# A down projection of 22 k-tiles rewritten as Strassen's seven block products

## The reference

```python
def conv_glu_ffn(h, w_up, conv_w, conv_b, w_down):
    a = h @ w_up
    ...
    gate, val = jnp.split(c, 2, axis=-1)
    return (jax.nn.silu(gate) * val) @ w_down
...
x = x + conv_glu_ffn(rmsnorm(x, ffn_norm_g[l]), ...)
```

## Time and profile before

| | us |
|---|---|
| median of three runs | 2753.74 |
| span of the profiled execution | 2752.7 |
| PE busy | 2696.4 |
| DVE busy | 1451.5 |
| POOL busy | 1127.4 |
| ACT busy | 1068.8 |

### The profile page before, as it was taken

One profiled execution on the slowest core, in us unless ns is written; L12 is line 12 of the kernel. 1 busy time (PEld: TensorE's weight loads), 2 busy tenths in 40 slices (PEclk: granted clock), 3 DMA queues, 4 the chain that ended last, 5 costly groups with the idle time before them and its releaser, 6 DMA issues.

```text
span 2752.7 us, 34759 instructions
## 1 busy us (share of the span) xinstructions
PE 2696.4 (98%) x13662; PEld 2197.4 (80%) x13662; DVE 1451.5 (53%) x2038; ACT 1068.8 (39%) x1614; POOL 1127.4 (41%) x625
## 2 busy tenths in 40 slices
PE   8999999999999999999999999999998999999998
...
GB/s 152 31 40 75 101 106 54 25 30 114 71 77 84 77 84 77 192 174 139 122 74 68 67 72 65 70 65 66 65 100 85 39 39 39 39 39 39 39 54 164
DMA packets 111787, 214.24 MB, mean 78 GB/s; under 512 B 32032, under 2 KB 61888, under 8 KB 111504
## 3 DMA queue, kind: packets, MB, share of 16 engines
...
q0 software_dynamic: 448, 1.88, 0.2%
...
## 4 chain that ended last, share of the span: by engine, by line
PE 88%; DVE 5%; ACT 2%; issue 2%; DMA 1%; POOL 1%; SPq 0%; ACTq 0%; DVEq 0%; POOLq 0%
PE gemm L1011 21%; PE gemm L1012 20%; PE gemm L1013 20%; PE small L1193 2%; PE small L1736 2%; PE small L1013 2%; PE small L1012 2%; PE small L1011 2%; PE small L1724 1%; PE small L1581 1%; PE gemm L1134 1%; PE small L1306 1%; PE small L1326 1%; PE gemm L1137 1%; PE gemm L1138 1%
## 5 line engine op out<-in xcount | busy, mean ns | idle before, releaser
L1011 PE MATMUL gemm<-h_hi,w_hi 128*128 128x512 f32 x2136 | 894.6, 419 | 22.7 <-DVE h_lo L2722 8.9
L1012 PE MATMUL gemm<-h_lo,w_hi 128*128 128x512 f32 x2136 | 845.1, 396 | 0.0
L1013 PE MATMUL gemm<-h_hi,w_lo 128*128 128x512 f32 x1960 | 776.6, 396 | 0.0
L819 POOL TENSOR_TENSOR w_hi<-w_raw,unit_col 128x1024 fp32r<-128x1024 f32 x134 | 262.6, 1960 | 1134.4 <-PE gemm L1013 891.6
L1011 PEld LDWEIGHTS gemm<-h_hi,w_hi 128*128 128x128 f32 x2136 | 403.9, 189 | 106.5 <-issue 11.2
L1012 PEld LDWEIGHTS gemm<-h_lo,w_hi 128*128 128x128 f32 x2136 | 404.3, 189 | 74.8 <-issue 2.9
L1013 PEld LDWEIGHTS gemm<-h_hi,w_lo 128*128 128x128 f32 x1960 | 369.3, 188 | 89.6
L828 POOL TENSOR_TENSOR w_lo<-w_raw,w_hi 128x1024 fp32r<-128x1024 f32 x118 | 305.3, 2587 | 13.8 <-DVE w_lo L2881 4.9
L972 POOL TENSOR_TENSOR w_hi<-w_raw,unit_col 128x1024 fp32r<-128x1024 f32 x32 | 60.8, 1899 | 310.9 <-PE gemm L1013 310.9
L3080 DVE TENSOR_TENSOR t_lo<-t_lo_f,t_hi 128x1024 fp32r<-128x1024 f32 x36 | 44.5, 1282 | 143.1 <-ACT t_hi L2238 143.1
L2541 ACT ACTIVATE xres<-xres,stat 128x128 f32<-128x128 f32 (+3 forms) x64 | 49.7, 777 | 151.0 <-DVE stat L3553 150.7
...
## 6 DMA issues: line engine op xcount, KB each, us to landing
w_raw<-w_stream SPq DMA_DIRECT2D x178, 512.0 KB, 3.5
t_lo_f<-act_spill SPq DMA_DIRECT2D x36, 512.0 KB, 4.4
act_spill<-taps SPq DMA_DIRECT2D x22, 512.0 KB, 2.9
x_spill<-xres ACTq DMA_DIRECT2D x16, 512.0 KB, 2.7
v_gate<-w_stream SPq DMA_DIRECT2D x11, 512.0 KB, 4.2
v_val<-w_stream SPq DMA_DIRECT2D x11, 512.0 KB, 3.4
xres<-x_t SPq DMA_DIRECT2D x8, 512.0 KB, 8.7
xres<-x_t ACTq DMA_DIRECT2D x8, 512.0 KB, 4.9
```

What stands on the lines that cost most here:

```text
L819: nc.gpsimd.tensor_tensor(whi[d][:, :, :], raw[s][:, :, :], unit, ALU.mult).then_inc(w_hi_done, 1)
L1011: mm(dst, w_hi, a_hi, start=first, stop=False, skip_group_check=onto)
L1012: mm(dst, w_hi, a_lo, start=False, stop=False, skip_group_check=onto)
L1013: return mm(dst, w_lo, a_hi, start=False, stop=last, skip_group_check=onto)
```

## The change

The down projection becomes one Strassen step over 2x2 blocks: the output features are cut in two halves, the tokens in two halves of 512, and the 22 k-tiles in 11 and 11. A unit `u` (0 to 10) is one k-tile of each half. There are seven block products. Each takes 11 units of 12 matmuls: four output tiles times the three of `dot3`, over 512 tokens. They run in four groups: two products side by side in groups 0, 1 and 2, one in group 3. TensorE goes (u, first), (u-1, second), (u+1, first), and so on, and keeps the first product's sums in four half banks (`A_BANKS`) and the second's in four others (`B_BANKS`). `unit_mm` counts finished units; the buffers of a unit are three deep, and most writes for unit n wait for `unit_mm` n-2, the end of unit n-3.

For each unit of groups 0, 1, 2, 3 POOL forms 1, 2, 1, 1 sums of weight blocks in place and 2, 1, 2, 0 low parts; ACT rounds each weight and each activation operand; DVE forms 1, 2, 1, 0 sums of activations, the low part of each activation operand in groups 0 to 2, and 0, 1, 0, 1 low parts of weights. In group 2 DVE also makes the sum and the low part for group 3's activations (`down_late_sum`, `down_late_low`). All of these are 128x512. At the end of each product `bank_add` adds each of four half banks to one or two places of `xres` (`TARGETS`). Weights are loaded anew for every group, 11, 17, 11 and 11 loads of 512 KB, into six buffers (four others in group 3); the activations are loaded once, in strips of 512 tokens. The GDN weights' first two splits wait for `unit_mm` 33.

```diff
+UNITS = FF_STEPS
+N_TWO = 3 * UNITS
+N_RAW, N_LATE = 6, 4
+W_SUMS, T_SUMS = (1, 2, 1, 1), (1, 2, 1, 0)
+POOL_LOWS, DVE_LOWS = (2, 1, 2, 0), (0, 1, 0, 1)
...
+        TARGETS = {(0, 0): ((C21, ALU.add), (C22, ALU.subtract)), (0, 1): ((C11, ALU.add), (C21, ALU.add)),
+                   (1, 0): ((C11, ALU.add), (C22, ALU.add)), (1, 1): ((C22, ALU.add),),
+                   (2, 0): ((C12, ALU.add), (C22, ALU.add)), (2, 1): ((C11, ALU.subtract), (C12, ALU.add)),
+                   (3, 0): ((C11, ALU.add),)}
+        ORDER = [(UNITS * g + u - part, part) for g in range(GROUPS - 1) for u in range(UNITS + 1) for part in range(2)
+                 if 0 <= u - part < UNITS]
...
+            def raw_load(j):
+                g, v, (i, a) = RAW_LOADS[j]
+                b, before = raw_of(j), raw_before(j)
+                if j < 2:
+                    sp.wait_ge(*prod_mm(PRODUCTS * (PAIRS - 2) + (3, 7)[j]))
+                elif j == 3:
+                    sp.wait_ge(*ff_scaled(2 * PAIRS))
+                elif j in (4, 5):
+                    sp.wait_ge(ff_prod, PAIRS)
+                if before is not None:
+                    _, used = units_of(*RAW_LOADS[before][0:2])
+                    sp.wait_ge(*w_a_ready(sums_to(POOL_LOWS, used)))
+                    if used > UNITS:
+                        sp.wait_ge(*w_b_ready(sums_to(DVE_LOWS, used)))
+                elif j >= N_EARLY:
+                    sp.wait_ge(*t_ready(t_place(2 * UNITS + CUT, 0)))
+                sp.dma_start(RAWS[b], w_stream[down_at(i, a)]).then_inc(raw_in[b].sem, 16)
...
+            act_load(R2, (0, 4), (SECOND[0], 0), b21_in[0])
+            raw_load(3)
             act_store(PAIRS - 1)
+            act_load(R2, (4, 8), (SECOND[4], 0), b21_in[1])
+            for j in (4, 5, 6, 7):
+                raw_load(j)
...
+            for n in range(N_UNITS):
+                g = n // UNITS
+                for half_row in SLABS[g]:
+                    raw_wait(n, *half_row)
+                if g == 0:
+                    down_sum(n, (0, 1), (1, 1), (0, 1), ALU.add)
+                elif g == 1:
+                    down_sum(n, (0, 0), (1, 1), (1, 1), ALU.add)
+                    down_sum(n, (0, 1), (0, 0), (0, 1), ALU.subtract)
+                elif g == 2:
+                    down_sum(n, (1, 0), (0, 0), (1, 0), ALU.add)
+                else:
+                    down_sum(n, (1, 0), (1, 1), (1, 0), ALU.subtract)
+                    continue
+                for part in range(POOL_LOWS[g]):
+                    pool.wait_ge(*w_rounded(2 * n + part + 1))
+                    nc.gpsimd.tensor_tensor(dw_low(n, part), dw_value(n, part), dw_hi(n, part).bitcast(F32), ALU.subtract).then_inc(w_a_ready.sem, 1)
+            pool.wait_ge(unit_mm, N_TWO)
...
+                    if u == 0 and g:
+                        bank_free(pe, g - 1, part, q)
+                    elif u == 0 and part == 0:
+                        pe.wait_ge(ff_prod, PAIRS - 1) if q < 2 else pe.wait_ge(*ff_scaled(2 * PAIRS))
+                    elif u == 0:
+                        pe.wait_ge(ff_prod, PAIRS - 1) if q < 2 else pe.wait_ge(*ff_scaled(2 * PAIRS - 1))
+                    last = dot3((A_BANKS, B_BANKS)[part][q], dw_hi(n, part)[:, q, :], dw_low(n, part)[:, q, :], dt_hi(n, part), dt_low(n, part),
+                                u == 0, u == UNITS - 1)
+                    if u == UNITS - 1 and (q < 3 or (part == 0 and g < GROUPS - 1)):
+                        last.then_inc(bank_mm.sem, 1)
...
+            for g in range(GROUPS):
+                for u in range(UNITS):
+                    unit_products(UNITS * g + u, 0)
+                    if u and g < GROUPS - 1:
+                        unit_products(UNITS * g + u - 1, 1)
+                if g < GROUPS - 1:
+                    unit_products(UNITS * g + UNITS - 1, 1)
...
+                    act.wait_ge(*prod_mm(PRODUCTS * (PAIRS - 1) + ((2, 4), (5, 6))[n][part]))
+                elif (n, part) == (2, 1):
+                    act.wait_ge(*ff_scaled(2 * PAIRS))
+                elif 3 <= n < N_TWO:
+                    act.wait_ge(unit_mm, n - 2)
+                elif n >= N_TWO:
+                    act.wait_ge(unit_mm, N_TWO - 1 if u < 3 else n - 2)
+                A(dw_hi(n, part), dw_value(n, part), ACT.Copy).then_inc(w_rounded.sem, 1)
...
+            down_t_high(0, 1)
             tap2(PAIRS - 1, 1)
+            down_w_high(2, 0)
+            down_t_high(2, 0)
+            down_w_high(2, 1)
+            down_t_high(1, 1)
             gate(PAIRS - 1)
+            for n in range(3, N_TWO):
+                g, u = divmod(n, UNITS)
+                if u == 0:
+                    down_t_high(n - 1, 1)
+                down_w_high(n, 0)
+                down_t_high(n, 0)
+                down_w_high(n, 1)
+                if u:
+                    down_t_high(n - 1, 1)
...
+                V.tensor_tensor(dt_value(n, part), left, right, op).then_inc(t_summed.sem, 1)
+                V.tensor_tensor(dt_low(n, part), dt_value(n, part), dt_hi(n, part).bitcast(F32), ALU.subtract).then_inc(t_ready.sem, 1)
...
+                V.tensor_tensor(dw_low(n, part), dw_value(n, part), dw_hi(n, part).bitcast(F32), ALU.subtract).then_inc(w_b_ready.sem, 1)
...
+                V.tensor_tensor(B21[u], B21[u], B22[u], ALU.add).then_inc(late_sum.sem, 1)
...
+                V.tensor_tensor(B21_r[u], B21[u], B22_r[u].bitcast(F32), ALU.subtract).then_inc(late_ready.sem, 1)
...
+                bank = (A_BANKS, B_BANKS)[part][q]
+                for i, ((m, c), op) in enumerate(TARGETS[g, part]):
+                    acc = xres[:, m + q, half(c)]
+                    ready = (g, part, i) in ((2, 0, 1), (3, 0, 0))
+                    V.tensor_tensor(acc, acc, bank, op).then_inc(down_ev if ready else bank_out.sem, 1)
...
+                    down_t_low(1, 0)
+                    down_t_sum(0, 1)
+                    down_t_low(0, 1)
                 tap(p, 0, 1)
                 tap(p, 0, 0)
+                if p == PAIRS - 1:
+                    down_t_sum(1, 1)
+                    down_t_low(2, 0)
                 tap(p, 1, 1)
+                if p == PAIRS - 1:
+                    down_t_low(1, 1)
                 tap(p, 1, 0)
                 product(p)
...
+            for n in range(3, N_TWO):
+                g, u = divmod(n, UNITS)
+                if u:
+                    down_t_sum(n, 0)
+                down_t_sum(n - 1, 1)
+                if u == 0:
+                    down_t_sum(n, 0)
+                    down_t_low(n - 1, 1)
+                down_t_low(n, 0)
+                if u:
+                    down_t_low(n - 1, 1)
+                if DVE_LOWS[g]:
+                    down_w_low(n)
+                if g == GROUPS - 2 and u >= 2:
+                    down_late_sum(u - 2)
+                if g == GROUPS - 2 and u >= 3:
+                    down_late_low(u - 3)
+                for part in range(2):
+                    if g and u == part:
+                        for q in range(4):
+                            bank_add(g - 1, part, q)
+            last = GROUPS - 2
+            down_t_low(N_TWO - 1, 1)
+            for u in range(UNITS - 2, UNITS):
+                down_late_sum(u)
+            down_w_low(N_TWO)
+            for u in range(UNITS - 3, UNITS):
+                down_late_low(u)
+            for q in range(4):
+                bank_add(last, 0, q)
+                if q % 2:
+                    down_w_low(N_TWO + 1 + q // 2)
+            for q in range(4):
+                bank_add(last, 1, q)
+                if q % 2:
+                    down_w_low(N_TWO + 3 + q // 2)
+            for u in range(5, UNITS):
+                down_w_low(N_TWO + u)
+                if u < 5 + KT // 2:
+                    lo_gained(u - 5)
+            for q in range(4):
+                bank_add(GROUPS - 1, 0, q)
+            for k in range(KT // 2, KT - 1):
+                lo_gained(k)
```

More of the change, by code:

```diff
@@ L107 @@
 IN_STREAM = 2 * PAIRS
+SKIP = IN_STREAM + 2 * FF_STEPS
 def up_at(u):
@@ L227, in build @@
         sum_w = sb("sum_w", [P, KT, 2])
+        w_ex = sb("w_ex", [P, KT, P], F32R)
+        with nc.sbuf_tensor("h_hi_f", [P, KT, S], F32) as hhi_f:
+            pass
         hhi = sb("h_hi", [P, KT, S], F32R)
@@ L258, in build @@
         H = sb("head", [P, 4, S])
+        with nc.sbuf_tensor("norm_r", [P, 4, S], F32R) as N_r:
+            pass
         N = sb("norm", [P, 4, S])
@@ new lines, in t_sums, with w_sums, bank_count @@
+        def t_sums(n, part):
+            return sum(summed(m // UNITS, at) for m, at in ORDER[:t_place(n, part)])
+        def w_sums(n, part):
+            g, u = divmod(n, UNITS)
+            return sum(W_SUMS[:g]) * UNITS + W_SUMS[g] * u + (1 + part if g == 1 else 1)
+        def bank_count(g, part, q):
+            done = 0
+            for key in TARGETS:
+                each = 1 if key == (2, 0) else len(TARGETS[key])
+                if key == (g, part):
```

(20 more changed lines are left out.)

371 lines of the change are left out of this document (235 added, 136 removed).

## The result

Four executions of the changed kernel gave 2778.07 to 2789.12 us, a median of 2783.21 us; four of the kernel before gave 2750.53 to 2758.90 us, a median of 2754.53 us. The ratio is 1.0101, 95% interval [1.0083, 1.0119]. The change makes the kernel 1% slower. The forecast of 2754.0 us was wrong, and the time lies above the range of 2734 to 2773 us. The medians differ by 28.7 us.

What follows compares the result with a forecast made beforehand. PE's matmul count bounds the stage, after the change DVE and POOL's turns in groups 1 and 2. Savings of 32.5 us against losses summed to +0.3 us on the span, so 2754.0 us; range 2734 to 2773 us.

Steps and rivals of the forecast that it cites:

- 132 matmuls fewer: Down projection: 924 matmuls stand for 1056, one every 0.2334 us, 30.8 us less.
- P (wait of 1.74 us gone): P, the end of the up products, moves from 1117.3 to 1115.6 as PE's wait for DVE goes: -1.7 us.
- start, clock with it: Start of the down projection: unit 4 late through product and loads, 9.4 us lost, plus 0.8 for a lower clock.
- group 1: Second group: DVE and POOL taking turns, 6.24 us a unit, 72.5 us against 61.6 of matmuls; loss 9.5 us.
- group 2: Third group: DVE and POOL taking turns, 70.1 us against 61.6 of matmuls; loss 8.5 us.
- border 2 to 3: From T, the end of group 2's last product: bank additions begin at T+0.4 and free banks late; loss 3.5 us.
- E to the norm's reciprocal: Behind E, the first GDN matmul: three lo_gained are left after the last matmul instead of one; loss 1.1 us.
- rival C: Group 3: weight loads late, turnover 13.5 us for 11.2, +7, 2761 us; chance 0.09 together with a start at its upper bound.
- A: Rival for groups 1 and 2: turns fit beside the matmuls, PE stays the bound; -15.2, 2738.5 us; chance 0.31.
- B: Rival for groups 1 and 2: DVE-POOL pairs cost full durations, 1.98 us; +21.7, 2775 us; chance 0.20, down to half its size.
- plus 1.2 as before: Group 2: 1.2 us added, as in group 1, for moments when DVE waits for ACT and POOL has nothing to do.
- 0.8 + 3 x 1.2: End of the stage: three lo_gained left put line 3134 at 4.3 us behind the last matmul, before 3.2; loss 1.1.

Runs made afterwards that it cites:

- Experiment 1: Changed kernel with POOL's sums and low parts in groups 1 and 2 a quarter as wide, the rest left out: 2750.68 us, 0.9979 of the kernel before.
- experiment 2: Changed kernel with DVE's down_late_sum ahead of down_t_low in group 2: 2776.37 us, 1.0065 of the kernel before.
- Experiment 7: Changed kernel with the last pair's taps and product ahead of units 1 and 2's sums and low parts, gate ahead of roundings: 2775.34 us, ratio 1.0069.
- Experiment 12: Changed kernel with late sum, last product and loads 4 and 5 earlier, own B21 semaphore, POOL's sums 34 to 36 held: 2769.05 us, ratio 1.0042.
- experiment 8: Changed kernel with the first two GDN weight tiles loaded early and split by POOL behind its fourth sum of group 3: 2785.12 us, ratio 1.0104.

## Why the prediction was wrong

The sum, step by step, on the profiled executions. At 0.2334 us a matmul a unit takes 5.60 us, a group of 22 products 61.62 us, and the 924 matmuls 215.7 us; P to E has 50.8 us more than that.

| term | forecast | measured |
|---|---|---|
| 132 matmuls fewer | -30.8 | -30.8 |
| P (wait of 1.74 us gone) | -1.7 | -4.3 |
| start, clock with it | +10.2 | +15.6 |
| rest of group 0 | 0 | +0.6 |
| group 1 | +9.5 | +12.9 |
| group 2 | +8.5 | +14.9 |
| border 2 to 3 | +3.5 | +6.9 |
| group 3 | 0 | -0.2 |
| E to the norm's reciprocal | +1.1 | +5.6 |
| all behind that | 0 | +2.4 |
| sum | +0.3 | +23.6 |

**What was right.** The matmuls kept their pitch but for 3% (0.231 us apart in group 0 without waits, 0.227 in group 3), the wait ahead of the last up product went, group 0 ran at the matmuls' pace, and in groups 1 and 2 the bound was DVE and POOL taking turns, 1.70 us a pair for the 1.68 of the forecast. Experiment 1 shows it: with short POOL operations 28.8 us went. Group 3 had no late loads, so rival C fell; A fell with the cycles of 6.5 and 7.1. B came nearest in time (2775), and group 2's 7.1 us is the prediction's own sign for it, but its mechanism is not what the rows show: a pair did not cost 1.98 us.

**Group 2, +6.4 over the forecast.** The step that failed is "plus 1.2 as before", the allowance for DVE waiting on ACT. It stood for the whole group; the trace has 0.70 + 0.35 us in every unit of the steady cycle, and 10.4 us in the group, as DVE asks for the low part right behind the sum that ACT must round first. DVE's waits from 1265 to 1339 us (total, times, longest):

```profile
DVE h_lo L3373 <- ACT h_lo L2485: 9.4, 17, 0.7
DVE head_r L3373 <- ACT head_r L2485: 1.0, 3, 0.3
```

The operations themselves took 6.06 us of the 7.10, less than the 6.24 of the forecast. Seven cycles of 7.10 for 6.24 us make 6.0 of the 6.4. The order of instructions on DVE decides this, and experiment 2 took 5.3 us out of P to E by it alone.

**Group 1, +3.4.** Here the allowance of 1.2 us was right: the trace has three waits of DVE for ACT, 1.0 us together, and none in most cycles. A unit took 6.50 us for 6.24 all the same: three pairs of 1.70 to 1.72 us, and 1.38 us for the two operations that were forecast at 0.60 each. A cycle of DVE's timeline, 1208.48 to 1215.00:

```profile
1208.48 1.79 DVE L3368 TENSOR_TENSOR h_lo_f<-h_hi_f,yt 128x512 f32<-128x512 f32 x1
1210.19 1.79 DVE L3368 TENSOR_TENSOR h_lo_f<-h_hi_f 128x512 f32<-128x512 f32 x1
1211.90 1.47 DVE L3373 TENSOR_TENSOR h_lo<-h_lo_f,h_lo 128x512 fp32r<-128x512 f32 x2
1213.28 1.79 DVE L3379 TENSOR_TENSOR norm_r<-norm,norm_r 128x512 fp32r<-128x512 f32 x1
```

Units 13 to 19 lost 1.8 us of the 3.4 against 6.24. The rest came at the ends of the group, above all where PE waited for bank additions and low parts in turn (units 11 and 12 took 5.58 and 9.54 us); no run separates the terms of the forecast there.

**Start, +5.4.** The product came at P+19.7 where the forecast had P+16, as three of the four taps met POOL's work (8.2 us for 5.1 alone) and a sum and two low parts stood between them, themselves 1.75 to 1.78 us long. This is the term that the prediction named as the least well known. Experiment 7 shows that order alone costs 6 us there. The forecast took 0.8 us for the clock. It cost about 3: behind the wait of 2.31 us it was 0.56 over 3.6 us, and the twelve matmuls there took 4.41 us for 2.80; behind that of 6.54 us it was 0.69 over 6 us, and the product took 4.22.

**Border, +3.4.** The forecast had the low part of unit 33 at about T-2.1 and the additions from T+0.4. They came at T+0.6 and T+3.0, 2.6 us late. The step that failed is that DVE and ACT would be on time: DVE's last late sums met POOL's four sums of group 3 (6.84 us), ACT waited 4.45 us for them before it could round them and then unit 33's weights, and DVE 1.22 us for that rounding. Experiment 12 shows it: with POOL held back the additions began at T+0.9, and the wait fell from 4.92 to 2.16 and 1.01 us. The product behind the wait took 5.26 us for 2.80, with the clock at 0.55, but the clock is hardly the cause: in experiment 12 it took 5.12 us at 1.00, as it had to wait for the additions that free its banks, a pair every 1.2 us.

**End, +4.5.** "0.8 + 3 x 1.2" took each `lo_gained` at its lone duration, although POOL's first GDN splits stand behind its sums of group 3 and a load and so land beside them: 5.98 us for three, as above. PE's wait rose from 0.22 to 3.77 us, 3.6 of the 5.6. The other 2.0 lie behind it, where the forecast had nothing: the clock was at 0.50, its lower level of 1.2 GHz, for 8 us, where the trace of before had 0.78 over 4 us. The reciprocal of the norm stands 24.21 us behind E for 18.59 before, and 19.85 in experiment 8, without the long wait. DVE's row of the kernel before and of the kernel after:

```profile
1382.42 0.20 DVE L3153 RECIPROCAL rstd_cols<-rstd_cols 128x8 f32<-128x8 f32 x1 [2.60 <-ACT rstd_cols L2308]
```

```profile
1403.66 0.20 DVE L3506 RECIPROCAL rstd_cols<-rstd_cols 128x8 f32<-128x8 f32 x1 [4.65 <-ACT rstd_cols L2581]
```

**What stays open.** P differs by 2.9 us among the thirteen profiles of the changed kernel and its variants (1112.99 to 1115.90), and the time behind the reciprocal by 6.0 us (1370.7 to 1376.7), though their instructions there are alike. So 2.6 and 2.4 us of the table are within what one execution scatters, and nothing was tried on them. But the one profile of before, with 1370.2 us behind the reciprocal, lies below all thirteen, so a small real loss there isn't ruled out. Nor are the 5 us explained by which the medians differ more than the profiled executions.

Start, border and end have a root in common: in each the trace has POOL's work beside DVE's where the forecast had less of it or none (8.2 us for 5.1, two late sums in 2.4 for 1.3, 5.98 for 3.67). Group 2 has another: an order of instructions in which DVE waits for ACT in each unit.
